# Ending a selection sooner: the order of the context's blocks, loads and elementwise steps around the first expert of a mixture layer

## The reference, cut to what matters

```
x1 = x + g1 * rmsnorm(m)                     # residual
h2 = rmsnorm(x1) * (1 + sc2) + sh2           # scaled and shifted normalised rows
aff = softmax(h2 @ w_router)                 # 16 experts
vals, idx = top_k(aff.T, cap)                # cap: 128 latent rows, 16 context rows per expert
hid = silu(h2[idx] @ w_gate) * (h2[idx] @ w_up)
out = (hid @ w_down) * vals                  # added back at rows idx, for each of 16 experts
y = x1 + g2 * rmsnorm(sum of out)
```

## Time and profile before

| | us |
|---|---|
| median of 3 runs | 2068.08 (2066.02 to 2070.84) |
| the profiled execution's own time | 2068.89 |
| its span, first to last instruction | 2067.2 |
| TensorE busy | 1991.6 (96%) |
| VectorE busy | 1173.7 (57%) |
| ScalarE busy | 754.4 (36%) |
| GpSimd busy | 278.3 (13%) |
| mean granted clock of TensorE | 0.988 |

### The profile page before, as it was taken

How to read it: one execution, slowest core, us unless ns; L and a number is a source line. 1 busy time by engine, 2 the same in 40 slices (tenths; PEclk the granted TensorE clock), 3 DMA queues, 4 the chain that set the end, 5 groups by cost and what they waited for, 6 DMA issues and landing times.

```text
span 2067.2 us, 32634 instructions
## 1 busy us (share of the span) xinstructions
PE 1991.6 (96%) x12705; PEld 1696.1 (82%) x12705; DVE 1173.7 (57%) x1618; ACT 754.4 (36%) x869; POOL 278.3 (13%) x279
## 2 busy tenths in 40 slices
PE   6999999999999999999999996799999999999996
PEld 4898989899999999998888785667777777777774
DVE  5655546485553332323224547767777777777766
ACT  7622221231111121111113431645555655555555
POOL 1010102010002000000000211211122111111215
PEclk9999999999999999999999998899999999999998
DMA  9011111224446111112335673588888877888889
GB/s 333 24 52 47 42 44 58 97 64 150 150 150 221 41 48 44 30 52 72 90 111 195 237 246 132 208 309 320 318 319 307 316 269 289 318 319 318 311 309 241
DMA packets 189545, 372.32 MB, mean 180 GB/s; under 512 B 11804, under 2 KB 110100, under 8 KB 188596
## 3 DMA queue, kind: packets, MB, share of 16 engines
q1 hardware_dynamic: 170272, 312.30, 41.8%
q0 software_dynamic: 19120, 59.29, 9.6%
q10 hardware_dynamic: 100, 0.03, 0.0%
HBM read 326.98 MB, written 43.03 MB: 179 GB/s over the span
## 4 chain that ended last, share of the span: by engine, by line
PE 79%; issue 7%; DVE 6%; DMA 4%; POOL 2%; ACT 1%; SPq 0%; POOLq 0%; DVEq 0%; ACTq 0%
PE ps L1068 8%; PE ps L1070 8%; PE ps L1069 8%; PE ps L1421 8%; PE ps L1403 8%; PE ps L1405 7%; PE ps L1412 7%; PE ps L1114 3%; PE ps L1115 3%; PE ps L1116 3%; PE ps L1080 2%; PE ps L1081 2%; PE ps L1082 2%; PE ps L1163 1%; PE ps L1164 1%
## 5 line engine op out<-in xcount | busy, mean ns | idle before, releaser
L2533 DVE TENSOR_TENSOR e_lo<-raw,e_hi 128x2048 fp32r<-128x2048 f32 x192 | 447.2, 2331 | 104.7 <-ACT e_hi L1897 99.8
L1897 ACT CAST e_hi<-raw 128x2048 fp32r<-128x2048 f32 x192 | 367.3, 1913 | 233.0 <-PE ps L1412 194.0
L1068 PE MATMUL ps<-h_hi,w_hi 128*128 128x384 f32 x744 | 249.4, 335 | 0.0
L1069 PE MATMUL ps<-h_lo,w_hi 128*128 128x384 f32 x744 | 248.6, 334 | 0.0
L1070 PE MATMUL ps<-h_hi,w_lo 128*128 128x384 f32 x744 | 248.6, 334 | 0.0
L2086 DVE TENSOR_TENSOR w_lo<-w_raw,w_hi 128x1024 fp32r<-128x1024 f32 x64 | 79.3, 1239 | 194.0 <-ACT w_hi L1599 192.8
L1403 PE MATMUL ps<-e_hi,x_hi 128*128 128x512 f32 x512 | 162.0, 398 | 5.0 <-DVE e_lo L2533 3.8
L1405 PE MATMUL ps<-e_lo,x_hi 128*128 128x512 f32 x512 | 159.5, 393 | 0.0
L1068 PEld LDWEIGHTS ps<-h_hi,w_hi 128*128 128x128 f32 x744 | 139.6, 188 | 3.3 <-issue 3.3
L1069 PEld LDWEIGHTS ps<-h_lo,w_hi 128*128 128x128 f32 x744 | 139.7, 188 | 0.0
L1070 PEld LDWEIGHTS ps<-h_hi,w_lo 128*128 128x128 f32 x744 | 139.7, 188 | 0.0
(11 more groups left out here) (354 smaller groups left out, 3724.2 us busy)
## 6 DMA issues: line engine op xcount, KB each, us to landing
raw<-in_w_gate_dram SPq DMA_DIRECT2D x64, 1024.0 KB, 8.5
raw<-in_w_up_dram SPq DMA_DIRECT2D x64, 1024.0 KB, 13.8
raw<-in_w_down_dram SPq DMA_DIRECT2D x64, 1024.0 KB, 11.6
w_raw<-in_w_in_dram SPq DMA_DIRECT2D x48, 512.0 KB, 4.1
ada_k<-in_w_ada_dram SPq DMA_DIRECT2D x32, 512.0 KB, 4.9
ada<-in_w_ada_dram SPq DMA_DIRECT2D x7, 1024.0 KB, 16.3
merged_d<-merged POOLq DMA_DIRECT2D x8, 576.0 KB, 6.2
ffn_d<-zero POOLq DMA_DIRECT2D x9, 512.0 KB, 7.1
```

The costliest lines, as they stand in the source:

```text
L1068: pe.matmul(out, w_hi[:, slot, k, :], xh, start=(k == 0), stop=False)
L1069: pe.matmul(out, w_hi[:, slot, k, :], xl, start=False, stop=False)
L1897: act.copy(e_hi[u % 4][:].rearrange("p k n -> p (k n)"), raw[(u + 8) % 12][:].rearrange("p k n -> p (k n)"))\
L2533: dve.tensor_tensor(e_lo[u % 4][:].rearrange("p k n -> p (k n)"), raw[(u + 8) % 12][:].rearrange("p k n -> p (k n)"), e_hi[u % 4][:].rearr ...
```

## The change

It re-orders lists on five engines, and moves two operations from GpSimd to VectorE; no arithmetic is changed but for the engine that does it.

TensorE: `turn_h2(7)`, its router steps and the transposes of the affinities go one to two context blocks forward; the fillers around the context's mix go from 12 and 8 to 10 and 6, and 6 new ones stand before the wait for the row numbers. In the first expert the context's transpose and router steps stand behind units 1, 2 and 3 (before: 3, 4 and 5), the transpose of its affinities behind unit 5 (before: 7), and the context products between the down units.

VectorE: `m_lo` comes after 8 rounds, not 11. The two operations on `h2_own` stand behind `low(0, 1)`; the context's selection stands behind `low(0, 7)`.

ScalarE: `square_ctx` and `scale_ctx` stand around `high(0, 1)`, before the gathered rows are cast; regrouping is a step of its own behind `high(0, 5)`.

GpSimd: the first gather stands behind the residual and the store of the context's rows. SP: the table and residual of the context are loaded ahead of unit 1.

```diff
@@ SP
+            sp.dma_start(tabs_c[:], tabs[:, 0:5:2, :]).then_inc(tabs_in[0], 16)
+            sp.dma_start(x_res_c[:], xp).then_inc(xr_in[0], 16)
             load_unit(0, 1, True)
-            sp.dma_start(tabs_c[:], tabs[:, 0:5:2, :]).then_inc(tabs_in[0], 16)
-            sp.dma_start(x_res_c[:], xp).then_inc(xr_in[0], 16)
@@ GpSimd
-            for b in range(2):
-                pool.wait_ge(h2_stored[b], 16 * 4)
-            pool.wait_ge(sel_read, 1)
-            gather_latents(0)
...
             pool.dma_start(yp, x1_c[:]).then_inc(x1_stored[0], 16)
+            for b in range(2):
+                pool.wait_ge(h2_stored[b], 16 * 4)
+            pool.wait_ge(sel_read, 1)
+            gather_latents(0)
             x1_deviation(8, 0)
-            pool.wait_ge(ctx_scaled, 2)
-            pool_steps.did(pool.tensor_tensor(h2_own[:], h2_own[:], tabs_c[:, 2, :], ALU.mult))
-            pool_steps.settle()
-            pool.tensor_tensor(h2_own[:], h2_own[:], tabs_c[:, 1, :], ALU.add).then_inc(h2_ready, 1)
@@ TensorE, context blocks
             ctx_block(2, 0)
+            turn_h2(7, 1)
             ctx_block(2, 1)
-            turn_h2(7, 1)
+            route_parts(7)
+            route(7)
             ctx_block(3, 0)
-            route_parts(7)
-            ctx_block(3, 1)
-            route(7)
-            pe.wait_ge(x1_ready, 8)
-            ctx_block(4, 0)
             pe.wait_ge(aff_done, NT - 1)
...
-            ctx_block(4, 1)
-            for j in range(5, CTX_UNITS):
+            ctx_block(3, 1)
+            pe.wait_ge(x1_ready, 8)
+            for j in range(4, CTX_UNITS):
...
-            keep_busy(6, 12)
+            keep_busy(6, 10)
             mix(8, 0, 0)
             mix(8, 0, 1)
-            keep_busy(6, 8)
+            keep_busy(6, 6)
@@ TensorE, first expert (new order)
+                for u in range(8):
+                    if u in (0, 2):
+                        pe.wait_ge(x_hi_done, u // 2 + 1)
+                    latent(0, u, u // 4 * 2, x_hi, x_lo, x_lo_done if u < 4 else None)
+                    if u == 1:
+                        turn_h2_ctx()
+                    elif u == 2:
+                        route_parts(8, h2T_c)
+                    elif u == 3:
+                        route(8)
+                    elif u == 5:
+                        pe.wait_ge(aff_done, NT)
+                        pe.transpose(ps[0:EXPERTS, 4, 0:P], aff[:, 0, 0, :], ident).then_inc(aff_turned, 1)
                 pe.wait_ge(sel_ready, 2)
...
                 for half in range(2):
                     turn_hidden(half, half + 1)
                 pe.wait_ge(sel_copied, 2)
...
+                turn_rows(1)
+                down(0, 8)
+                down(0, 9)
...
                 for u in range(4):
                     context(u, 4, 0, xc)
+                down(0, 10)
                 for u in range(4, 8):
                     context(u, 7, CAP_Q, xc)
+                down(0, 11)
@@ ScalarE, first expert
+                square_ctx()
                 high(0, 1)
+                scale_ctx()
                 high(0, 2)
                 high_rows(0)
                 high(0, 3)
-                square_ctx()
                 high(0, 4)
-                scale_ctx()
+                ctx_features()
                 high(0, 5)
+                out_of_parts(8)
+                regroup_ctx()
                 high(0, 6)
-                ctx_features()
+                exp_logits(8)
                 high(0, 7)
-                out_of_parts(8)
                 gate_latents(0)
-                exp_logits(8)
-                for u in range(8, 12):
-                    high(0, u)
+                high(0, 8)
+                high(0, 9)
+                high(0, 10)
                 high_hidden(0)
+                high(0, 11)
@@ VectorE
-            select(*latents, range(11))
+            select(*latents, range(8))
             dve.wait_ge(m_hi_done, NT)
             dve.tensor_tensor(m_lo[0][:], m_ctx[:], m_hi[0][:].bitcast(F32), ALU.subtract).then_inc(m_lo_done, 1)
-            select(*latents, range(11, CAP_L // 8), ends=True)
+            select(*latents, range(8, CAP_L // 8), ends=True)
...
                 low(0, 0)
                 low(0, 1)
+                dve.wait_ge(ctx_scaled, 2)
+                did(dve.tensor_tensor(h2_own[:], h2_own[:], tabs_c[:, 2, :], ALU.mult))
+                settle()
+                dve.tensor_tensor(h2_own[:], h2_own[:], tabs_c[:, 1, :], ALU.add).then_inc(h2_ready, 1)
                 low(0, 2)
                 low_rows(0)
...
+                top_logit(8)
+                low(0, 6)
+                affinities(8)
+                low(0, 7)
+                select_context()
                 low(0, 8)
-                affinities(8)
+                hidden_latents(0, 1)
+                copy_context()
+                rows_of_context()
+                low_hidden(0)
                 low(0, 9)
-                hidden_latents(0, 1)
-                select_context()
-                low_hidden(0)
+                turn_context(0)
                 low(0, 10)
-                copy_context()
+                low_rows(1)
                 low(0, 11)
-                rows_of_context()
-                low_rows(1)
-                turn_context(0)
-                dve.wait_ge(sel_read, 6)
-                scale_latents(0)
                 hidden_context(0, 3)
                 turn_context(1)
-                for u in range(3):
-                    low(1, u)
+                dve.wait_ge(sel_read, 6)
+                low(1, 0)
+                scale_latents(0)
+                low(1, 1)
+                low(1, 2)
                 out_context(0)
@@ VectorE, ret_merge: the low part ahead of the wait for the rows
+                    if k == KD - 4:
+                        split(T_RETOUT, 2, n, 2)
                     if k % 2 == 0:
                         dve.wait_ge(ada_k_in[k // 2 % 2], 32 * n + 16 * (k // 4) + 16)
...
-                    if k == KD - 4:
-                        split(T_RETOUT, 2, n, 2)
```

More of the change, by code:

```diff
@@ L1446, in first_expert @@
                 pe.transpose(ps[0:CAP_C, 4, 144:160], sel_f[0:EXPERTS, CAP_L:CAP], id16).then_inc(sel_turned, 1)
[L1447 removed]
+                for half in range(2):
+                    turn_hidden(half, half + 1)
                 pe.wait_ge(sel_copied, 2)
                 pe.matmul(ps[:, 7, 0:2 * EXPERTS], flip[0:CAP_C, P:2 * P], sel_c[:], start=True, stop=True).then_inc(sel_flipped, 1)
[L1450 to L1451 removed]
+                turn_rows(1)
+                down(0, 8)
+                down(0, 9)
                 pe.wait_ge(sel_read, 6)
```

27 lines of the change are left out of this document (5 added, 22 removed).

## The result

| | before | after |
|---|---|---|
| median of 4 runs each, taken in turn | 2067.93 (2066.02 to 2070.84) | 2048.19 (2047.88 to 2050.02) |
| span of the profiled execution | 2067.2 | 2046.2 |
| TensorE's mean granted clock | 0.988 | 0.992 |

The ratio is 0.9905, with a 95% interval of 0.9888 to 0.9922: 19.7 us less. A repeat in five rounds gave 2048.18 and 0.9909 (0.9896 to 0.9923). The forecast was 2048.6. So the sum was right; whether its terms were is what the rest is about.

A forecast was written before the change was run, and what follows sets the result against it. TensorE bounds the kernel outside one window, 1238 to 1388 us, where it waits and runs at reduced clock. Terms 4.0 + 10.6 + 4.9 = 19.5 us off 2068.9 gave 2049.4, or 2048.6 against the median; range 2043 to 2058.

The forecast's parts named there:

- The view of the whole: One window, 1238 to 1388 us, has waits to give; TensorE bounds the kernel before and behind it.
- Second term: Inside the first expert: waits 7.0 and half-speed spells 4.6 go, 1.0 of new waits comes; 10.6 us gained (6 to 12.5).
- Third term: Second expert's first eight units: weights requested earlier, so TensorE no longer waits for them; 4.9 us gained (3 if DMA is taken).
- The rival in which the DMA takes back the end: DMA queue full from 1330 to about 1365; Third term and some 3 us of Second term lost, 2056; chance 0.07.
- First term: Selection, context's mix and first gather: gathered rows and first product come earlier, 4.0 us gained (1.0 to 6).
- `ret_merge`, 0 predicted: Low part moved ahead of the wait for `w_ada` rows: TensorE, busy throughout there, hides either order; 0 us.
- That the context's chain is what the first gather waits for: Rival: late table and slow descriptors make First term about 0, with 2 us of follow-up waits; 2055; chance 0.18.
- Half speed all through the expert: Rival: waits keep TensorE at 1.2 GHz through the first expert; up to 13 us slower, 2081; chance 0.04.
- That nothing moves: Rival: gather not earlier and new waits replace those removed, so all three terms fail; 2067 to 2069; chance 0.03.

## Why the prediction was right, and where its terms were not

**The view of the whole** held. But for 1 us in `ret_merge` only the window had time to give; behind it everything moved as a block (from the second expert's context products to the end 679.2 us before, 679.4 after). The waits removed are those named, and no DMA bound took their place.

**Second term, 10.6 predicted, 11.05 measured** (63.81 to 52.76). Idle time fell by 6.3 where 7.0 less 1.0 was said, busy time by 4.7 where 4.6 was said for the half-speed spells. It was worked out by adding two kinds of rows, waits and clock, and both kinds came out, though not item by item. Of the waits, 1.0 for `hcT` and 0.4 for `x_lo` went as well, which I had not counted; `hid` kept 0.6, and new are 1.1 for `hT_hi`, ScalarE's high part of the hidden rows, and 0.5 for a low part. Of the clock, the spell at the expert's start was in no term: it took 5.24 us at 0.64 before and takes 2.48 at 0.60 now, behind 10 us of waiting. By the clock it was cut by 0.9 (5.24 x 0.36 less 2.48 x 0.40, an estimate), so the 4.7 holds more than the two spells of the sum, and part of the agreement is luck. The reason given for the wait for `h2_own` was wrong in part: I credited its going to VectorE, but with GpSimd in the new order it is gone as well.

**Third term, 4.9 predicted, 4.7 measured** (26.7 to 22.0), by the mechanism named: SP asked for the second expert's first units at 1329.5 instead of 1350.9, 15 us before TensorE wanted them. The rival in which the DMA takes back the end is out: the share is 1.03 there, and TensorE is busy all the time.

**First term, 4.0 predicted for the window, 2.3 measured.** This is the term that was mis-sized. The first product came 5.4 us earlier, 3.1 of which were there before the window. With those 3.1 taken off the predicted times, the steps compare so: mix end 1266.6 predicted, 1266.54 measured; tables there 1272.9 and 1274.7; residual ready 1278.9 and 1279.6; gather issued 1279.9 and 1280.8; rows landed 1288.1 and 1290.1. So the mix's end is right to 0.1 us. (Two sums on the way were not: 1239.3 less 3.8 plus 0.6 is 1236.1 for the affinities and not 1236.6, and eight rounds behind 1258.5 end at 1276.7, not 1276.2; neither is what released the mix.) The step that failed is the landing of the tables: from the bounds of 5.1 and 9.6 I took 6.2, by their size against a lone unit, and it needed 7.9 or 8.0 in all ten profiled executions that have it ahead of unit 1 (9.4 to 9.6 in the four that have it behind). What was wrong is that the bytes of this copy were priced like the bytes of a unit. The stretch of its landing in the kernel after:
```profile
1266.73:1274.73 8.00, 3.68 (x17) 2.92 (x16) 6.41 (x17) 2.23 (x3) 0.75 (x2) 0.93 0.83 223
```
The engines moved 1.77 MB in it, of which the copy is 1.57, so the loads issued behind it took little. Their share was 1.04 from 1268.5 to 1270.5 and 1.00 in the 2 us behind, at 305 and 270 GB/s; full shares of weights move 407. This copy, from SBUF to SBUF, keeps the engines busy at a lower rate; why is open. Nor was the 5.1 of the earlier trace rows a lone transfer: in the 1.7 us before that issue the DMA share was 1.07. The estimate by the fit of the Trainium skill ("DMA: Bandwidth & Descriptors", Anatomy of one DMA), 5.6, was further off still; the page gives that fit for transfers issued from GpSimd, and this one is issued from SP.

The second step that was off is the gather itself: 9.3 instead of 8.1 from issue to landing. The longer issue, left inside the range as 0.6, was 0.8 (1.89 less 1.11), but it is not the whole reason: with issues of 1.08 the landing took 8.5, 9.2 and 9.3 in three runs. One more thing in the traces goes with it. From the end of the issue to the landing it takes 6.4 to 7.0 us in the five traces in which the store of the context's rows (512 KB) does not stand ahead of the gather, and 7.0 to 8.2 in the nine in which it does. The DMA share during the gather is 1.02 before and after. That the store takes its share ahead of the gather is thus a likely part of the 1.2, but not shown: in the one run that moved the store alone, the issue grew by 1.0 as well. What gave part of it back was the undisturbed add: the residual was ready 4.9 us after the tables and not the 6.0 that I took.

The lower bound of this term, 1.0, was too high by its own working: 4.0 less 3.4 for a table at 9.6 and 1.2 for an unlucky add is -0.6. The run with the tables behind unit 1 is that case (a table of 9.4, an add of 4.20): its gathered rows come 2.9 later than after, so its first term is about -0.5.

**The issue beside low parts.** With no low part at work the gather's issue takes 1.08 us (in the runs with 11 rounds, with unit 1 first, with fillers alone); beside low parts 1.89, 2.26, 2.53 and 3.22. The Trainium skill ("SBUF — State Buffer", SBUF: two separate sides) has the pair of ports shared by the two engines as a lock that is held for a whole instruction, also by a VectorE operation with two inputs in SBUF when the GpSimd operation reads SBUF. The durations agree: in the kernel with fillers the low part that began at 1276.08 beside the multiply ended at 1280.06, and the add, begun at 1278.05, needed until 1282.26, which is 2.2 after it. Its box on descriptors names only VectorE's two-port modes; these rows show the issue longer beside two-input subtractions too.

**`ret_merge`, 0 predicted, about 1.0 measured.** I read only the stretch of 470 to 705, in which TensorE never stops. The wait for `ada_acc` stood in another place, where the sum of the first round is needed, and the waits of the whole span would have shown it. A cover read in one stretch was taken for all rounds.

**Sum.** By the two traces: 3.1 before the window, 2.3 + 11.05 + 4.7 inside, -0.2 behind it, 21.0. Predicted: 19.5. Without the 2.1 of luck ahead of the window the terms make 18.9, which is what the repeat's medians gave (18.8). So the total was hit in part by luck: a shortfall of 1.7 in the first term met 1.0 of `ret_merge` that I had not counted, and 0.4 too little in the second.

**Rivals.** That the context's chain is what the first gather waits for is true, and the run with the tables behind unit 1 shows what it costs when it ends late: 3.3 us in the median, not the 6.4 of the rival, as the second term did not suffer. Half speed all through the expert did not come: a clock of 0.60 for 2.5 us, then 1.00. That nothing moves is out.

## What to carry to other kernels

When two chains meet at one engine, look at which small step in a queue is earliest in both: here one VectorE pass, moved three selection rounds forward, carried 9.7 us beside the other edits, while the two operations that changed their engine carried nothing. Time a half-clock spell as idle time and busy time apart, from one row of a stretch each, since covering the idle time with fillers gives the second back only if nothing in the hand-over shifts with it. Where two engines share the memory, the order in which two large passes start decided some 2 us here (an add of 2.34 or 4.2): fix it with a wait instead of leaving it to chance.

## What the runs showed of the hardware

- An operation of VectorE on 128x16 values with two inputs took 2.20 us instead of 0.17 because GpSimd's pass over 128x1024 had begun 0.17 us earlier. In the five traces in which it began behind such a pass, it ended within 0.04 us of that pass's end.
- The same copy of 1.5 MB inside SBUF took 7.9 to 8.0 us with nothing ahead of it and 9.4 to 9.6 behind 1 MB of weights: what stood ahead explains some 1.5 us of its time, not 3 or more. It kept the DMA engines at a share of 1.00 to 1.04 while they moved 270 to 305 GB/s; weights moved 407 at 1.03.
- The gather of the rows landed 6.4 to 7.0 us after the end of its issue in the five traces without a 512 KB store ahead of it, and 7.0 to 8.2 after it in the nine with one.
- VectorE's wait for the landing of `tabs`, earlier in the kernel, lay between 1.6 and 5.0 us from execution to execution, with no edit near it, and what stands behind it came at times 2.4 us apart in ten traces of kernels that are alike up to there.
